# Moving parts of VectorE's work in the differential attention to ScalarE and GpSimd, and giving y's split its own buffers

## The reference

```
z = h @ w_in                                   # one input projection, split into parts
q_d, k_d = rope(dq), rope(dk)                  # latent tokens; 4 heads x 2 maps x 64
p = softmax(q1 k1) - lam * softmax(q2 k2)      # differential attention, per head
o_d = rms(p @ v_d) * (1 - lam_init)
y = g_m*(o_m @ w_m) + g_a*(o_a @ w_a) + g_d*(o_d @ w_d)   # g = sigmoid(gate_pre)
x = x + g1 * (y @ w_out)
```

## Time and profile before

| | us |
|---|---|
| median of 3 runs | 2632.36 |
| the profiled execution, its own time | 2634.0 |
| its span | 2632.2 |
| PE busy | 2533.6 (96%) |
| DVE busy | 1250.5 (48%) |
| ACT busy | 750.8 (29%) |
| POOL busy | 1330.7 (51%) |

### The profile page before, as it was taken

How to read it: one execution, slowest core, us unless ns; L and a number is a source line. 1 busy time by engine, 2 the same in 40 slices (tenths; PEclk the granted TensorE clock), 3 DMA queues, 4 the chain that set the end, 5 groups by cost and what they waited for, 6 DMA issues and landing times.

```text
span 2632.2 us, 41789 instructions
## 1 busy us (share of the span) xinstructions
PE 2533.6 (96%) x17328; PEld 2367.1 (90%) x17328; DVE 1250.5 (48%) x1699; ACT 750.8 (29%) x1373; POOL 1330.7 (51%) x607
## 2 busy tenths in 40 slices
PE   5999999999999999999989999999999999999997
PEld 3989986888899999999978899778888999999997
DVE  5443255866735423132554523659565363132235
ACT  3251355213322303021222513550334123112031
POOL 2535530453356666666654466106434666666664
PEclk8999999999999999999998999999999999999999
DMA  6202224531121222222211122342111222222221
GB/s 262 71 22 68 73 103 161 189 117 41 41 73 65 73 76 77 72 74 80 73 64 49 36 68 74 127 165 71 64 41 49 72 73 73 72 81 73 73 75 63
DMA packets 62556, 215.34 MB, mean 82 GB/s; under 512 B 6688, under 2 KB 11168, under 8 KB 62112
## 3 DMA queue, kind: packets, MB, share of 16 engines
q1 hardware_dynamic: 56448, 203.97, 22.7%
q10 hardware_dynamic: 5920, 8.70, 0.9%
HBM read 208.15 MB, written 4.49 MB: 81 GB/s over the span
## 4 chain that ended last, share of the span: by engine, by line
PE 84%; DVE 7%; issue 3%; ACT 2%; POOL 1%; DVEq 1%; DMA 1%; SPq 1%; POOLq 0%; ACTq 0%
PE big L517 21%; PE big L520 21%; PE big L521 21%; PE four L703 3%; PE big L774 3%; PE four L786 2%; PE four L599 2%; PE four L805 2%; PE big L543 1%; PE big L726 1%; PE big L546 1%; PE big L547 1%; PE four L746 1%; DVE prob_d L1651 1%; DVE prob_d L1649 1%
## 5 line engine op out<-in xcount | busy, mean ns | idle before, releaser
L481 POOL TENSOR_TENSOR w_hi<-raw,cst 128x1024 fp32r<-128x1024 f32 x288 | 552.8, 1919 | 1177.5 <-PE big L517 886.6
L517 PE MATMUL big<-act_hi,w_hi 128*128 128x320 f32 x2528 | 790.3, 313 | 6.6 <-issue 5.6
L520 PE MATMUL big<-act_lo,w_hi 128*128 128x320 f32 x2528 | 785.3, 311 | 0.0
L521 PE MATMUL big<-act_hi,w_lo 128*128 128x320 f32 x2528 | 785.1, 311 | 0.0
L484 POOL TENSOR_TENSOR w_lo<-raw,w_hi 128x1024 fp32r<-128x1024 f32 x288 | 742.7, 2579 | 41.0
L517 PEld LDWEIGHTS big<-act_hi,w_hi 128*128 128x128 f32 x2528 | 478.6, 189 | 16.0 <-issue 14.7
L520 PEld LDWEIGHTS big<-act_lo,w_hi 128*128 128x128 f32 x2528 | 478.6, 189 | 0.7
L521 PEld LDWEIGHTS big<-act_hi,w_lo 128*128 128x128 f32 x2528 | 478.3, 189 | 0.0
L517 PE MATMUL big<-u_hi,w_hi 128*128 128x320 f32 (+1 forms) x1024 | 319.0, 312 | 1.9 <-DVE u_lo L2071 1.9
L520 PE MATMUL big<-u_lo,w_hi 128*128 128x320 f32 (+1 forms) x1024 | 317.4, 310 | 0.0
L521 PE MATMUL big<-u_hi,w_lo 128*128 128x320 f32 (+1 forms) x1024 | 317.1, 310 | 0.0
(11 more groups left out here) (306 smaller groups left out, 3832.8 us busy)
## 6 DMA issues: line engine op xcount, KB each, us to landing
raw<-in_w SPq DMA_DIRECT2D x368, 512.0 KB, 3.4
first_mod<-in_first SPq DMA_DIRECT2D x16, 512.0 KB, 15.7
x<-in_x ACTq DMA_DIRECT2D x1, 2560.0 KB, 13.1
out_y<-x SPq DMA_DIRECT2D x8, 320.0 KB, 2.6
cst<-in_const ACTq DMA_DIRECT2D x1, 1664.0 KB, 7.8
small<-in_small ACTq DMA_DIRECT2D x2, 437.0 KB, 9.2
out_C<-c_new ACTq DMA_DIRECT2D x2, 258.0 KB
v_d<-in_past ACTq DMA_DIRECT2D x2, 256.0 KB, 2.9
```

Of the source, the lines that this page charges most:

```text
L481: nc.gpsimd.tensor_tensor(w_hi[:, to, :], raw[:, slot, :], ones[:, 0:1].to_broadcast([P, BLK]), ALU.mult)
L517: first = mm(ps, wh, ah, start=k == 0, stop=False)
L520: mm(ps, wh, al, start=False, stop=False)
L521: last = mm(ps, wl, ah, start=False, stop=k == nk - 1)
```

## The change

Five edits, all of them in both layers:

1. dq and dk: ACT, behind its copy to `stage`, writes the four crossed groups of 32 partitions to `crossed` (rs or sq) and the context tokens to q_d or k_d; DVE does the sine product in one instruction of 128 partitions. The first `keep_row` of the next layer moves from behind tile 4's copy to ahead of it.
2. attend_d: the second map is scaled by ACT (`scale_second`); DVE only multiplies its factor, a column, by -lambda. The output copy moves to ACT.
3. `turn` waits for the output copy only before its fifth transposition.
4. The add of a gated half branch to y moves from DVE to POOL, which does the four of pair p ahead of splitting the second gate block of pair p+1.
5. y's split: tiles 0 to 5 get buffers of their own, ACT rounds 0 to 3 behind gate 3, 4 and 5 behind gate 5, 6 and 7 behind gate 7, and DVE writes remainder m-1 behind tile m.

```diff
         stage = sb("stage", [P, 2, T])
+        crossed = [rs, sq[:, 0, :]]
...
         prob_d = at("prob_d", [P, 4, T], A0 + 34816)
-        tanh_d = [stage[:, 0, :], stage[:, 1, :], prob_d[:, 2, :], prob_d[:, 3, :]]
+        tanh_d = [stage[:, 0, :], stage[:, 1, :], prob_d[:, 0, :], prob_d[:, 1, :]]
+        y_hi, y_lo = at("y_hi", [P, 6, T], A0 + 41088, f32r), at("y_lo", [P, 6, T], A0 + 56448, f32r)
+        def y_tile(k):
+            return (y_hi[:, k, :], y_lo[:, k, :]) if k < 6 else (act_hi[:, k, :], act_lo[:, k, :])
...
+            def add_half_branches(l, p):
+                for item in range(4):
+                    m, h = divmod(item, 2)
+                    z = slice(h * HALF, (h + 1) * HALF)
+                    pool.wait_ge(half_merged, l * 16 + 4 * p + item + 1)
+                    nc.gpsimd.tensor_tensor(y[:, 2 * p + m, z], y[:, 2 * p + m, z], t1[:, z], ALU.add).then_inc(half_added, 1)
+                    if h:
+                        pool.drain().then_inc(y_done, 1)
+                for p in range(4):
+                    if block == FIRST_BLOCK["merge_a"] + 3 * p + 4:
+                        add_half_branches(l, p)
...
                     pe.wait_ge(p_ready, l * 60 + 40 + i + 1)
-                    if i:
-                        pe.wait_ge(out_copied, l * 20 + i)
                     for c in range(1 if t == LATE else 5):
+                        if c == 4 and i:
+                            pe.wait_ge(out_copied, l * 20 + i)
...
                     pe.wait_ge(pT_copied, l * 60 + 40 + i + 1)
+                    if t == LATE:
+                        pe.wait_ge(out_copied, l * 20 + i)
...
-                project(l, USE["wout"], FIRST_BLOCK["wout"], 8, KD, act_hi, act_lo,
-                        arrived=lambda k: l * SPLITS + FIRST_SPLIT["y"] + k + 1)
+                project(l, USE["wout"], FIRST_BLOCK["wout"], 8, KD, None, None,
+                        arrived=lambda k: l * SPLITS + FIRST_SPLIT["y"] + k + 1, tile=y_tile)
...
-            def round_tiles(l, name, pairs, scale=None):
+            def round_tiles(l, name, pairs, scale=None, only=None):
                 for k, (hi, src) in enumerate(pairs):
+                    if only is not None and k not in only:
+                        continue
...
+                def scale_second(i):
+                    h, t = units[i]
+                    w, c1 = CTX if t == LATE else T, 2 * (i % 2) + 1
+                    act.wait_ge(second_factor, l * 20 + i + 1)
+                    f(prob_d[:, c1, 0:w], prob_d[:, c1, 0:w], ACT.Copy, scale=row_sum[:, c1:c1 + 1]).then_inc(second_scaled, 1)
+                def outputs(i):
+                    h, t = units[i]
+                    q0, q1 = queries(t)
+                    act.wait_ge(o_ready, l * 60 + 40 + i + 1)
+                    f(q_d[:, h, q0:q1], out_d[i % 2], ACT.Copy).then_inc(out_copied, 1)
                 for i in range(-1, n):
+                    if i >= 1:
+                        outputs(i - 1)
                         copyT(i)
+                    if i + 1 < n:
+                        scale_second(i + 1)
                         head_square(l, (i - 6) // 5)
+                outputs(n - 1)
+                act.drain()
...
                     use = USE["dq"][m]
+                    if l + 1 < DEPTH and m == 4:
+                        keep_row(l + 1, 0, one[0][:, 0:256])
                         .then_inc(free[b], 1)
+                    act.drain()
+                    dst = q_d[:, m, :] if m < 4 else k_d[:, m - 4, :]
+                    for g in range(4):
+                        r, o = slice(32 * g, 32 * g + 32), slice(32 * (g ^ 1), 32 * (g ^ 1) + 32)
+                        f(crossed[m % 2][o, CTX:T], stage[r, m % 2, CTX:T], ACT.Copy)
+                    f(dst[:, 0:CTX], stage[:, m % 2, 0:CTX], ACT.Copy)
                     act.drain().then_inc(raw_kept, 1)
-                    if l + 1 < DEPTH and m in (4, 7):
-                        keep_row(l + 1, m // 7, one[0][:, 0:256])
+                    if l + 1 < DEPTH and m == 7:
+                        keep_row(l + 1, 1, one[0][:, 0:256])
...
                     head_hi(l, "od", q_d, od_hi, h)
-                for m in range(2, 8):
-                    gate_of_d(l, m)
-                round_tiles(l, "y", [(act_hi[:, k, :], y[:, k, :]) for k in range(KD)], scale=0.5)
+                y_pairs = [(y_tile(k)[0], y[:, k, :]) for k in range(KD)]
+                for gates, rounded in (((2, 3), range(0, 4)), ((4, 5), range(4, 6)), ((6, 7), range(6, 8))):
+                    for m in gates:
+                        gate_of_d(l, m)
+                    round_tiles(l, "y", y_pairs, scale=0.5, only=rounded)
...
             def merge_d(l, behind):
+                dve.wait_ge(half_added, l * 16 + 16)
...
                     dve.wait_ge(half_ready[h], l * 16 + 4 * p + 2 + m + 1)
+                    if 4 * p + item - 4 >= 2:
+                        dve.wait_ge(half_added, l * 16 + 4 * p + item - 4 - 1)
                     dve.drain().then_inc(half_merged, 1)
-                    last = v.tensor_tensor(y[:, 2 * p + m, z], y[:, 2 * p + m, z], t1[:, z], ALU.add)
-                    if h:
-                        last.then_inc(y_done, 1)
-                    dve.drain()
...
                     p0, p1 = (prob_d[:, 2 * (i % 2) + m, 0:w] for m in range(2))
-                    v.tensor_scalar(p1, p1, row_sum[:, c0 + 1:c0 + 2], neg_lam, ALU.mult, ALU.mult)
-                    dve.drain()
+                    v.tensor_scalar(row_sum[:, c0 + 1:c0 + 2], row_sum[:, c0 + 1:c0 + 2], neg_lam, None, ALU.mult)\
+                        .then_inc(second_factor, 1)
+                    dve.wait_ge(second_scaled, l * 20 + i + 1)
-                def outputs(i):
-                    h, t = units[i]
-                    q0, q1 = queries(t)
-                    dve.wait_ge(o_ready, l * 60 + 40 + i + 1)
-                    v.tensor_copy(q_d[:, h, q0:q1], out_d[i % 2]).then_inc(out_copied, 1)
                 for i in range(-1, n + 1):
-                    if i >= 1:
-                        outputs(i - 1)
...
                     v.tensor_tensor(t1[:, CTX:T], src[:, CTX:T], c_("cos_d"), ALU.mult)
-                    for g in range(4):
-                        r, o = slice(32 * g, 32 * g + 32), slice(32 * (g ^ 1), 32 * (g ^ 1) + 32)
-                        v.tensor_tensor(t2[o, CTX:T], src[r, CTX:T], c_("sin_d", r), ALU.mult)
-                    v.tensor_copy(dst[:, 0:CTX], src[:, 0:CTX])
+                    v.tensor_tensor(t2[:, CTX:T], crossed[m % 2][:, CTX:T], c_("sin_d"), ALU.mult)
...
-                    for k in range(0, 6) if m == 5 else ([m] if m > 5 else []):
+                    for k in {0: (), 7: (6, 7)}.get(m, (m - 1,)):
                         dve.wait_ge(hi_done, l * SPLITS + FIRST_SPLIT["y"] + k + 1)
-                        v.scalar_tensor_tensor(act_lo[:, k, :], y[:, k, :], 0.5, act_hi[:, k, :].bitcast(f32),
+                        v.scalar_tensor_tensor(y_tile(k)[1], y[:, k, :], 0.5, y_tile(k)[0].bitcast(f32),
...
-        sign = [z, -z] if name == "d" else [-z, z]
-        put("sin_" + name, np.tile(np.concatenate(sign), (P // dim, 1)))
+        put("sin_" + name, np.tile(np.concatenate([-z, z]), (P // dim, 1)))
     put("mask_b", np.where(q <= p, 0.0, NEG))

```

More of the change, by code:

```diff
@@ L344, in trunk @@
         half_ready, half_free = [sem("half_ready_a"), sem("half_ready_b")], [sem("half_free_a"), sem("half_free_b")]
-        half_gated, half_merged = sem("half_gated"), sem("half_merged")
+        half_gated, half_merged, half_added = sem("half_gated"), sem("half_merged"), sem("half_added")
         out_copied = sem("out_copied")
@@ L373, in trunk @@
         scaled, squared = sem("scaled"), sem("squared")
+        second_factor, second_scaled = sem("second_factor"), sem("second_scaled")
         x_scaled = sem("x_scaled")
@@ L497, in block_start, with project @@
                 pe.wait_ge(split_ready, l * DENSE + b + 1)
-            def project(l, uses, first_block, tiles, nk, hi, lo, n=HALF, arrived=None, more=0):
+            def project(l, uses, first_block, tiles, nk, hi, lo, n=HALF, arrived=None, more=0, tile=None):
                 for p in range(tiles * nk):
@@ L515, in project @@
                         wh, wl = w_hi[:, slot, col:col + P], w_lo[:, slot, col:col + P]
-                        ah, al = hi[:, k, h * n:h * n + z], lo[:, k, h * n:h * n + z]
+                        if tile:
+                            ah, al = (a[:, h * n:h * n + z] for a in tile(k))
+                        else:
+                            ah, al = hi[:, k, h * n:h * n + z], lo[:, k, h * n:h * n + z]
                         first = mm(ps, wh, ah, start=k == 0, stop=False)
```

## The result

The changed kernel takes 2595.41 us (median of 4 runs, 2593.68 to 2596.14), against 2632.30 before: a ratio of 0.9858, 95% interval 0.9841 to 0.9875. I had said 2606, and 2595 to 2619; the gain is 36.9 us where 26.3 were forecast. The sign came as written, and so did most of the mechanisms; the term for attend_d did not, and the gain that I added up was three tenths too small. One of the 21 runs of the kernel before in the later series took 13925.36 us: the median of its seven, 2633.2, counts it, the ratios do not.

The account below looks back on a forecast made before the run. PE, 96% busy, was taken as the bound, with only its stands and the clock behind them to gain. Terms 6.0 + 1.3 + 6.4 + 13.3 = 27.0 us took the median 2632.4 to 2605.4, stated as 2606, range 2595 to 2619.

Parts of the forecast that it names:

- the term for attend_d: attend_d, both layers: shorter waits of PE and clock regained, 13.3 us gained, bounds 5 and 17.3.
- What bounds the kernel: Whole kernel: PE works 96% of the span; only its standing time and the clock lost behind it can be gained.
- dq and dk, keep_row: Second layer's dq and dk gain 6.0 us from a shorter stand and clock; the earlier keep_row gains 1.3 us.
- wout: Start of wout, both layers: y's tiles ready earlier, 3.2 us a layer, 6.4 together.
- The walk: Start of wout: add to y caught by POOL, remainder 6 late, PE waits 1.3 us 36 products in.
- rival B: Everything hides: attend_d gains 17.3 us, wout 9.4, the others as forecast; 34.0 us, 2598; chance 0.17.
- the factor at 0.2 us: Sign in attend_d: the factor's instruction L1702 near 0.2 us on the mean speaks for rival B, near 1 for Rival A.
- (a): attend_d: turn's 7.7 us wait for the output copy falls to waits for L1651, only where both instructions are caught.
- (b): attend_d: the 8.3 us wait of values, put down to late maxima, goes but for new collisions.
- (d): attend_d: L703's 2.6 us and the scores' 1.3 us of waits stay, since L1618 stands behind L1651 as before.
- Rival A: attend_d: factor nearly always caught, L1651 again behind it; perhaps 6 of 16.0 us go, no clock; 2613; chance 0.22.
- The clock: attend_d: 14 products behind the 2.51 us wait took 3.33 us in place of 2.06; 1.3 us comes back.

Follow-up runs that it names:

- e10: Changed kernel, but VectorE again does the four crossed sine products and the context copy of dq and dk; the earlier keep_row stays: 2603.92 us.
- e1: Changed kernel, but VectorE scales the second softmax map again (640 columns) in place of ScalarE: 2603.35 us.
- e8: Changed kernel, but the factor -lambda is multiplied onto two columns, written to scratch columns, in place of one: 2596.64 us.
- e3: Changed kernel, but VectorE adds the gated half branches to y again in place of GpSimd: 2606.24 us.
- e4: Changed kernel, but turn waits for ScalarE's output copy of the unit before ahead of its first transposition: 2595.42 us.
- e2: Changed kernel, but VectorE does the output copy again, ahead of maxes; turn still waits before its fifth transposition: 2595.39 us.
- e6: Changed kernel, but both the scaling of the second map and the adds to y are back on VectorE: 2615.29 us.
- e7: Changed kernel, but the output copy is back on VectorE and turn waits for it ahead of its first transposition: 2594.32 us.
- e5: Changed kernel, with an unread VectorE reduction over the same half of t1 where VectorE's add to y used to be: 2596.37 us.
- e11: Kernel before the change, but GpSimd adds the half branches to y and the first keep_row comes early: 2620.88 us.
- e9: Changed kernel, but all eight tiles of y are split into act_hi and act_lo as before, rounded behind gate 7: 2601.71 us.

## Where the prediction was right, and which step failed

*What bounds the kernel* held: all of the gain is PE's standing time and the clock behind it.

*dq and dk, keep_row.* 6.0 and 1.3 us forecast, 6.6 and 1.4 found by the stages, and e10 gives both apart. My fear that three instructions would each wait out POOL was wrong in a harmless way: one per tile is caught, and in none of the 16 tiles of both layers does a GpSimd instruction overlap the two behind it.

*wout.* 6.4 us forecast, 7.8 found. The walk was right step by step: the add to tile 7 is caught, remainder 6 is late, and PE stands 36 products in. It stood 0.59, not 1.3 us, chiefly because POOL was through its second instruction 5.3 us behind wout's first product (796.84 to 802.14), where I had 5.8; the first remainder ended 0.7 us behind that, near the 0.8 that I had let it (timeline).

```profile
799.34 2.80 POOL L505 TENSOR_TENSOR w_lo<-raw,w_hi 128x1024 fp32r<-128x1024 f32 x1
...
800.06 3.50 DVE L2094 SCALAR_TENSOR_TENSOR act_lo<-y,act_hi 128x640 fp32r<-128x640 f32 x2 [0.18 <-issue]
...
802.88 0.41 PE L541 MATMUL big<-act_hi,w_hi 128*128 128x320 f32 x1 [0.59 <-DVE act_lo L2094]
```

*attend_d* is the step that failed: "16.0 - 4.0 + 1.3 = 13.3 us. Bounds 5 and 17.3". Measured is 21.3. That the total still fell inside 2595 to 2619, by 0.4 us, is luck and no support for this term: the lower end came from rival B, which let everything hide. B comes nearest in its total (2598), and its sign, the factor at 0.2 us, is there; but its 17.3 us for attend_d are 4.0 short too, and its 9.4 us for wout are too many. Three errors, all to the low side:

1. *What stays.* I left 4.0 us of (a) and (b) and, in (d), the 2.6 and 1.3 us of L703 and the scores. Measured is 3.1 us of listed waits, three per layer (0.67, 0.47, 0.41 in the first), from 20.0: 16.9 us gone where I had 12.0. Of the 16.0 us of (a) and (b) 0.9 were left, not 4.0. (d) was right for the scores, whose 1.3 us stayed, and wrong in saying that L1618 stays late because it stands behind L1651: the lateness was the pile-up of caught instructions, and with fewer of them the waits of this line (L727 now) shrank to 0.8 us in total. The wait of 0.92 us that went comes back in both layers of e1, and one of 0.86 in e8, but not in e3: it belonged to the scaling and its factor. Rival A's condition, that the factor is caught, did not hold, and e8 shows what decides it.
2. *What a stand costs.* I took a listed wait for its cost. It is counted from the modelled end of the product before, 0.31 us after its start where the next one follows after 0.147, and the first product behind it is slower. In the earlier trace rows the wait reads 1.30 us, but the starts lie 1.61 us apart:

```profile
616.38 0.31 PE L703 MATMUL four<-act_hi,w_lo 128*128 128x320 f32 x1
617.99 1.38 PE L746 MATMUL four<-probT_d,v_d 128*128 128x128 f32 x10 [1.30 <-ACT probT_d L1164]
```

   Over the kernels whose attend_d shows no fall of the clock, the stage less its listed waits grows with their number: 139.0 to 139.2 us at 3 waits (changed, e4), 139.9 at 5 and at 7 (e3 in the second layer, e1), 140.6 at 10 (before, second layer), so about 0.22 us for each over the whole range. Single steps are uneven: one more stand in e2 (139.6 at 4) and two more in e3 and e8 (139.9 to 140.1 at 5) cost 0.4 to 0.5 each. From 19 to 6 thirteen stands went, by this slope an estimate of 2.9 us that no term held. With the 1.8 us that went from (d) it is also why the upper bound was no bound.
3. *The clock* gave 1.5 us (the first layer before, 142.0 less 139.1 and six stands of 0.22), forecast 1.3. The two layers of e3, and those of e6, have equally many stands and the low clock in the first alone; less their waits they differ by 1.6 us each, which bears this out.

16.9 + 2.9 + 1.5 = 21.3 us, which is what the stage gained. Measured in this sum are the 16.9 and the 4.4 beside them; how these divide into 2.9 and 1.5 is my estimate, and that the sum closes does not test it.

*Which edit does it.* I had put 7.7 us down to the output copy, as the wait's releaser. e2 and e7 give it 1.6 us at most, and e4 nothing. The scaling is worth 9.2 us by the stages and the adds 10.3, and e5 shows that it is not VectorE's time but being held up by GpSimd. So the cause that I read from the earlier trace rows was right, and the bookkeeping by releaser wrong: it named who came last, not what had made him late.

*The adds on GpSimd.* e11 shows this edit to gain 10.4 us without the scaling and the output copy, although the add takes 876 ns there and 493 undisturbed on VectorE. The GPSIMD Engine Reference of the Trainium skill (Engine selection) keeps an elementwise add off GpSimd; I wrote that this changes nothing in the sum. By that rule the edit should cost time or gain nothing, and the measurement decides against it here.

*Who is caught.* An instruction of VectorE with two SBUF inputs is held up (L1675, 1069 ns on the mean in e3); one that reads PSUM (L1672, 485) or reduces (L1678, 486) is not. The page SBUF — State Buffer of the Trainium skill (SBUF: two separate sides), which I had weighed for rival A, has the lock on the shared port pair against instructions with two SBUF inputs or in a two-port mode, and these rows agree. Of the factor, one column took at most 216 ns and two columns up to 2453. The page Advanced Engine Details and Errata of the Trainium skill (VectorE Performance Modes) asks, for the two-port mode at 2x, for source and destination in SBUF and for an even count in their most non-unit major dimension, or an odd one over 1 that is equal in both. Both rows agree with it.

## What to carry to other kernels

Where GpSimd streams beside a VectorE that must be on time, count VectorE's instructions on the critical path that are longer than their undisturbed twins (here those with two SBUF inputs, the scaling of 640 columns and the factor of two), and move those first, to ScalarE or even to GpSimd itself in a gap of its own; the ones that read PSUM, reduce, or write one column were never caught here and may stay. Do not price an edit by the releaser that a wait names: follow the late engine's timeline back to the first instruction that is longer than its undisturbed twin. And add to every listed wait of TensorE what the interruption itself costs (an estimate of 0.2 to 0.5 us here), by timing the stage from first product to first product. Compare such stage times rather than totals where the effect is a few microseconds.

## What the runs showed of the hardware that I had not expected

- A VectorE TENSOR_SCALAR of one column ran at 212 to 216 ns in 40 of 40 cases, 24 of which overlap a GpSimd instruction; of two columns 16 were caught, up to 2453 ns (e8).
- Whether the instruction behind a caught one is caught too depends on what GpSimd does then. L2068 (677 to 687 ns) and L2070 (691 to 695 ns) never are, though L2067 ahead of them took up to 2902, but GpSimd was idle beside them in 16 of 16 tiles. Before, L1649 was caught 12 times with 640 columns, and in 6 of these L1651 behind it as well, as in the earlier trace rows.
- ScalarE's copy of 32 x 512 across partition groups took 627 to 632 ns, and with a per-partition scale 640 columns took 820 (L1199) against 740 with a constant one (L1129, y's rounding).
- The length of TensorE's stand alone does not tell whether the granted clock falls between its levels of 2.4 and 1.2 GHz. In attend_d stands of up to 1.6 us left it alone in every run. One of 1.86 us (e3, first layer), of 2.23 us (e6) and of 2.51 us (before) lowered it in the first layer, while the second layer's of the same length did not. The 2.81 us ahead of wout lowered it in both layers before and in e11, and in neither of e9.
